# Both V gathers of a pair issued together in the gather phase of a hybrid decoder step

## The chip, the cores and the metric

The kernel runs on one core of one Trainium2 chip. The metric is the device time of one execution in microseconds. The program is one launch; its engines are PE (TensorE, matmuls), DVE (VectorE), ACT (ScalarE), POOL (GpSimd) and SP (SyncE, here only an issuer of DMAs). Each has its own instruction stream, and semaphores order them against each other.

## What is computed

One layer of a decoder trunk for 1024 prompt tokens and 8 sample tokens, model width 1024. A mixer (an SSD head group and an mLSTM head group) gives `x1`; then comes PEER, a layer that picks 128 experts (8 heads x 16) for each token out of 16384, and each expert is one row of `peer_u` and one row of `peer_v`:

```python
def _peer(x, wq, keys, u, v):            # cut to what matters
    ...
    eidx = jnp.take_along_axis(cidx, pos, axis=-1)      # 128 expert numbers per token
    gate = jax.nn.softmax(top, axis=-1)
    hid = gelu(einsum('td,thkd->thk', xb, jnp.take(u, eidx, axis=0)))
    return einsum('thk,thkd->td', gate * hid, jnp.take(v, eidx, axis=0))
...
x1 = _layer_norm(ALPHA * x + mix, ln1_g, ln1_b)
x2 = _layer_norm(ALPHA * x1 + _peer(x1, ...), ln2_g, ln2_b)
```

All is fp32. A row of `peer_u` or `peer_v` has 1024 numbers, 4 KB.

## The kernel before

Three parts run one after the other: the input projections and convolutions, the two scans with the output projection, and `build_peer`, which holds the change. Its first gather starts 967 us after the start of the span.

**Tiles of tokens.** The prompt is cut into 8 tiles of 128 tokens, the samples are a ninth. Five tiles (`GATHERED = 5`) are done by gathering: for one expert column of one tile, an indirect DMA fetches 128 rows, one for each token, into a buffer of 128 x 1024 (512 KB). The other three tiles are done densely: all of `peer_u` and `peer_v` pass in 128 blocks of 128 rows, with the gates of unpicked experts at zero.

**Slots.** The gather work is written as a loop over slots `t`, unrolled on each engine. Slot `t` handles the U column `t` (tile `t // 128`): POOL gathers the rows into `ub[t % 4]` (line 1597), and DVE multiplies them with the token's `x1` and sums (line 1833, the "dot" of the slot, semaphore `dot`). After 16 columns ACT takes the gelu and DVE multiplies the gate in (`wg`). 16 to 20 slots later the V column is gathered into `vbf[v % 4]` (`gather_v`, line 1572) and added with its weight.

**Two ways for V.** Up to slot 319 (`SD = 320`) V column `v = t - 20` is handled in slot `t`, so V columns 0 to 299 (`PE_ROWS = 300`), and PE does the sum: two columns make a pair, with half of the tokens of each in either buffer half, and in each odd slot PE multiplies the two rows of the pair with small diagonal matrices `dg` that ACT prepared and adds into PSUM (lines 2194 to 2206, semaphore `pv`, one count for each pair). That "V product" is 8 matmuls in the trace. From slot 320 on, DVE adds V rows itself (line 1873), and PE works on the dense blocks.

**Waits on POOL.** POOL issues its gathers in the order of the loop and each waits for its buffer. A U gather of slot `t` waits for the dot of slot `t - 4` (line 1593). A V gather `v` below 300 waits, through `v_free(v - 4)`, for the product of the pair to which `v - 4` belongs (line 1568):

```python
if 0 <= v < PE_ROWS:
    pool.wait_ge(s["pv"], v // 2 + 1)
```

As POOL's stream is in order, a gather that waits holds back all gathers behind it.

**Other work of these slots.** `background(t)` lays the mixing product, the normalisation, the scores and the top-16 picks of the coming tiles over the slots, in stretches of 36: PE does `mix` (line 2122) and `score` (line 2140), DVE the norm and the picks (lines 1620 to 1742). From slot 246 on, for slots up to 318, one-hot products build the gates of the dense tiles (`one_hots`, PE line 2248). SP loads what this needs, and from slot 300 on the first dense blocks.

Of the kernel before, what the change touches and what calls it, by code (L numbers as in the profile page):

```python
# [73 lines left out]
def free(eng, sem, value):  # L74

    if not isinstance(value, int) or value > 0:
        eng.wait_ge(sem, value)


def build(nc, a, o):  # L80
# [17 lines left out]
    with top:  # L98
# [451 lines left out]
        with ExitStack() as ctx:  # L550
            build_scan(nc, a, o, ctx, sem, PB, ident, two, wo, s_wo, s_pre, pre, mt0, cht_d, chs_d, tok_d, rows_d, rows_s_d, bc_d, mixt_d)
        end_phase()
        build_peer(nc, a, o, locals())


# [631 lines left out]
def build_peer(nc, a, o, L_):  # L1187
# [20 lines left out]
    LAG, LAG_PE, SD = TOPK, TOPK + 4, 320  # L1208
    PE_ROWS = SD - LAG_PE
# [17 lines left out]
    def v_rows(t):  # L1227

        if t < LAG_PE:
            return ()
        if t < SD:
            return (t - LAG_PE,)
        if t < SD + LAG_PE - LAG:
            v = PE_ROWS + 2 * (t - SD)
            return (v, v + 1)
        return (t - LAG,)

    def by_dve(v):  # L1240

        return max(0, v - PE_ROWS)
# [19 lines left out]
    with ExitStack() as ctx:  # L1262
# [106 lines left out]
        with nc.Block() as block:  # L1369
            @block.sync  # L1370
            def _(sp):
# [152 lines left out]
                for b in range(NBLK):  # L1524
                    if b + 4 < NBLK:
                        load_u(b + 4)
                    if b + 7 < NBLK:
                        load_v(b + 7)
                    if b % 8 == 1 and 8 < b < NBLK - 8:
                        load_g(b // 8 + 1)  # L1530
                    if block_slot(b) <= 386 < block_slot(b + 1):
                        sp.wait_ge(s["dot"], 3 * CH)
                        sp.wait_ge(s["acc0"], 1)
                        load_x1g(4)
                    if block_slot(b) <= 408 < block_slot(b + 1):
                        sp.wait_ge(s["ax"], by_dve(3 * CH))
                        load_gix(4)
                    if block_slot(b) <= 420 < block_slot(b + 1):
                        sp.wait_ge(s["pick"], NP - 1)
                        sp.wait_ge(s["mixg"], 4 * NP - 3)  # L1540
                        sp.wait_ge(s["x1st"], 16 * PICK[SAMPLE])
                        for n in range(3):
                            load_xs(n)
                    if block_slot(b) <= 560 < block_slot(b + 1):
                        sp.wait_ge(s["dot"], 4 * CH)
                        sp.wait_ge(s["acc0"], 3)
                        load_xs(3)
                        sp.wait_ge(s["stored"], 16 * 4)
                        load_xs(4)
# [7 lines left out]
            @block.gpsimd  # L1557
            def _(pool):
                nc.gpsimd.iota(iou, [[1, P]], 0, 0).then_inc(s["iou"], 1)
                pool.wait_ge(s["iou"], 1)  # L1560

                def gather(buf, table, index, done):
                    pool.indirect_dma_start(out=buf, out_offset=None, in_=a[table],  # L1563
                                            in_offset=bass.IndirectOffsetOnAxis(ap=index, axis=0)).then_inc(done, 16)

                def v_free(v):
                    if 0 <= v < PE_ROWS:
                        pool.wait_ge(s["pv"], v // 2 + 1)
                    elif v >= 0:
                        pool.wait_ge(s["ax"], by_dve(v + 1))  # L1570

                def gather_v(v):
                    n, h, k = v // CH % 2, v % CH // TOPK, v % TOPK
                    m, e = k // 2, k % 2
                    if v < CH and v % 32 == 0:
                        pool.wait_ge(s_gixv[0], 64 * (v // 32 + 1))
                    elif v % CH == 0 and v < PE_ROWS:
                        pool.wait_ge(s_gixv[n], 64 * (1 if n else 5))
                    v_free(v - NB)
                    pool.sem_inc(s["passed"], 1)  # L1580
                    at = 64 * e + 8 * h + m
                    gather(vbf[:, v % NB, :], "peer_v", (gixv if v < PE_ROWS else gixu)[n][:, at:at + 1], s_v[v % NB])

                for t in range(SLOTS):
                    c, h, k = t // CH, t % CH // TOPK, t % TOPK
                    if t < CH and t % 32 == 0:
                        pool.wait_ge(s["ix0"], t // 32 + 1)
                    if 0 < c < GATHERED and t % CH == 0:
                        pool.wait_ge(s_gix[c % 2], 16 * (c // 2 if c % 2 == 0 else (c + 1) // 2))
                    if t == U_SLOTS:  # L1590
                        pool.wait_ge(s["trc"], 1)
                    if t < U_SLOTS + NSMP:
                        free(pool, s["dot"], t - 3)
                    pool.sem_inc(s["passed"], 1)
                    if t < U_SLOTS:
                        at = 64 * (k % 2) + 8 * h + k // 2
                        gather(ub[:, t % NB, :], "peer_u", gixu[c % 2][:, at:at + 1], s_u[t % NB])
                    elif t < U_SLOTS + NSMP:
                        gather(ub[:, t % NB, :], "peer_u", ixs[:, t - U_SLOTS:t - U_SLOTS + 1], s_u[t % NB])
                    for v in v_rows(t):  # L1600
                        gather_v(v)
                    if t in (290, 292, 294, 296):
                        k = (t - 290) // 2
                        if k == 0:
                            pool.wait_ge(s["xdh"], 1)
                        nc.gpsimd.tensor_tensor(xds[:, 1, 2 * k:2 * k + 2, :], xraw[:, 2 * k:2 * k + 2, :],
                                                xds[:, 0, 2 * k:2 * k + 2, :].bitcast(f32), ALU.subtract).then_inc(s["xdlo"], 1)
                for b in range(NSMP):
                    if b < NB:
                        v_free(U_SLOTS - NB + b)  # L1610
                    else:
                        pool.wait_ge(s["dot"], U_SLOTS + NSMP)
                    pool.sem_inc(s["passed"], 1)
                    gather((vbf if b < NB else ub)[:, b % NB, :], "peer_v", ixs[:, b:b + 1], s_vs[b])

            @block.vector
            def _(dve):
# [126 lines left out]
                def norm2(r, step):  # L1744
                    y = acc[r]
                    if step == 1:
                        free(dve, s["ax"], by_dve((r + 1) * CH))
                        V.bn_stats(st7[:, 0, :], y[:, 0:512])
                        ch.link_plain(V.bn_stats(st7[:, 1, :], y[:, 512:D]))
                    elif step == 2:  # L1750
                        ch.link(V.bn_aggr(mv7[:, :], st7[:, :, :]))
                        V.tensor_scalar(mv7[:, 1:2], mv7[:, 1:2], EPS, None, ALU.add).then_inc(s["yvar"], 1)
                    elif step == 5:
                        dve.wait_ge(s["ysq"], r + 1)
                        ch.link(V.reciprocal(mv7[:, 1:2], mv7[:, 1:2]))
                    elif step == 7:
                        dve.wait_ge(s["gl1"], 32)
                        V.scalar_tensor_tensor(y, y, mv7[:, 0:1], gb1[:, :], ALU.subtract, ALU.mult).then_inc(s["ymul"], 1)
                        dve.wait_ge(s["ymul"], r + 1)
                    elif step == 12:  # L1760
                        dve.wait_ge(s["gl2"], 32)
                        V.scalar_tensor_tensor(y, y, mv7[:, 1:2], gb2[:, :], ALU.mult, ALU.add).then_inc(s["y"], 1)
# [594 lines left out]
```

## Time and profile before

| | us |
|---|---|
| median of 3 runs (3498.75 to 3521.03) | 3500.99 |
| span of the profiled execution | 3505.5 |
| first U gather | 967 |
| first and last V gather for PE | 1033.5 and 2113.2 |

| engine | busy us of the span | share |
|---|---|---|
| PE | 3153.1 | 90% |
| DVE | 2539.3 | 72% |
| POOL | 1752.3 | 50% |
| ACT | 951.9 | 27% |

The profile is of one execution. Times count from the start of its span. A gather on POOL (`DMA_INDIRECT`) is busy only while POOL makes its descriptors; the data moves afterwards, in the DMA engines, and its landing is seen where the engine that needs it starts. In a row of the view in order of time, the square bracket gives the idle time of the engine before the row and what ended it by the profile. "issue" means that nothing the profile shows was waited for.

### The profile page before, as it was taken

The numbers are of one execution on the slowest core, as the hardware profiler recorded it, in microseconds if no ns is written. First come the engines' busy times: TensorE is split into PE (matmuls) and PEld (weight loads), VectorE is DVE, ScalarE is ACT, GpSimd is POOL, SyncE is SP. The second block draws the span as 40 slices with busy tenths as digits, with TensorE's granted clock in tenths as the row PEclk, the third lists the DMA queues.
The fourth block names the chain that finished last, engine by engine and source line by source line (L and its number), as shares of the span: only waits on it lengthen the run. The fifth ranks groups of instructions, "written<-read, shape, count | busy, mean of one in ns | idle before, by whom it ended". The sixth has DMA issues, their size and how long they took to land.

```text
span 3505.5 us, 42684 instructions
## 1 busy us (share of the span) xinstructions
PE 3153.1 (90%) x13863; PEld 2084.0 (59%) x13863; DVE 2539.3 (72%) x5317; ACT 951.9 (27%) x2199; POOL 1752.3 (50%) x1420
## 2 busy tenths in 40 slices
PE   8989999999788888888868676999999999999998
PEld 8987887787332233233334345776676766767764
DVE  6662001799486888888899996777777777877777
ACT  3112222566111111111158882111111111111111
POOL 3341221344034666667665565555555555555553
PEclk9999999999899999999989888999999999999999
DMA  4324433788667999999998999999999999999996
GB/s 147 92 68 161 154 139 117 270 278 300 247 208 265 340 352 355 352 338 341 343 344 323 351 331 392 384 394 390 379 389 399 391 371 365 395 401 388 389 377 241
DMA packets 385327, 1074.38 MB, mean 306 GB/s; under 512 B 55128, under 2 KB 145144, under 8 KB 378848
## 3 DMA queue, kind: packets, MB, share of 16 engines
q0 software_dynamic: 186624, 679.56, 51.8%
q1 hardware_dynamic: 146592, 308.65, 24.4%
q10 hardware_dynamic: 51904, 83.63, 6.5%
q8 instruction: 102, 1.67, 0.2%
q14 instruction: 105, 0.86, 0.1%
HBM read 978.52 MB, written 93.05 MB: 306 GB/s over the span
## 4 chain that ended last, share of the span: by engine, by line
PE 41%; DMA 12%; DVE 8%; issue 7%; POOL 4%; ACT 2%; POOLq 0%; ACTq 0%; DVEq 0%
PE PB L2177 17%; PE PB L2164 14%; DMA vbf<-in_peer_v,gixv 6%; DMA x1d<-in_peer_u 4%; PE PB L2153 3%; PE PB L2204 3%; PE PB L2140 2%; DVE ub L1833 2%; POOL ub L1563 2%; DMA ub<-in_peer_u,gix 2%; POOL vbf L1563 2%; PE PB L2248 1%; ACT oha L1988 1%; PE PB L2122 1%; DVE ohb L1780 1%
## 5 line engine op out<-in xcount | busy, mean ns | idle before, releaser
L1563 POOL DMA_INDIRECT ub<-in_peer_u,gix x640 | 707.8, 1106 | 641.6 <-DVE hid L1833 432.8
L2177 PE MATMUL PB<-vbd,wd 128*128 128x512 f32 x1536 | 686.5, 597 | 0.0
L2164 PE MATMUL PB<-xds,uts 128*128 128x384 f32 x3072 | 569.4, 340 | 0.0
L2164 PEld LDWEIGHTS PB<-xds,uts 128*128 128x128 f32 x3072 | 531.7, 189 | 0.5 <-issue 0.5
L1563 POOL DMA_INDIRECT vbf<-in_peer_v,gixv x300 | 341.9, 1140 | 273.5 <-PE PB L2204 138.3
L1563 POOL DMA_INDIRECT vbf<-in_peer_v,gix x340 | 397.3, 1169 | 160.8 <-issue 98.7
L2177 PEld LDWEIGHTS PB<-vbd,wd 128*128 128x128 f32 x1536 | 284.6, 192 | 310.7 <-issue 310.7
L2204 PE MATMUL PB<-vbf,dg 128*64 128x512 f32 x1200 | 329.9, 673 | 136.6 <-DMA vbf<-in_peer_v,gixv 126.3
L1794 DVE TENSOR_TENSOR uts<-PB,uts 128x512 fp32r<-128x512 f32 x256 | 176.1, 688 | 304.7 <-ACT uts L2010 285.9
L1833 DVE CUSTOM_DVE_ANT_0 ub<-ub,x1g 128x1024 f32<-128x1024 f32 x257 | 313.7, 1223 | 79.0 <-DMA ub<-in_peer_u,gix 65.4
L2010 ACT CAST uts<-PB 128x512 fp32r<-128x512 f32 x256 | 150.3, 587 | 650.2 <-PE PB L2153 631.9
L1833 DVE CUSTOM_DVE_ANT_0 ub<-ub,x1gb 128x1024 f32<-128x1024 f32 x256 | 311.7, 1217 | 4.8 <-DMA ub<-in_peer_u,gix 4.6
L2204 PEld LDWEIGHTS PB<-vbf,dg 128*64 128x64 f32 x1200 | 88.4, 147 | 322.3 <-issue 312.3
L1873 DVE SCALAR_TENSOR_TENSOR acc<-vbf,wg,acc 128x1024 f32<-128x1024 f32 x212 | 271.3, 1280 | 4.8 <-DMA vbf<-in_peer_v,gix 3.7
L2140 PE MATMUL PB<-wp,x1T 128*128 128x512 f32 x576 | 270.7, 613 | 1.2 <-ACT x1T L1962 1.2
L2122 PE MATMUL PB<-wo,mt 128*128 128x512 f32 x528 | 248.9, 616 | 12.4 <-DVE x L1624 6.0
L2140 PEld LDWEIGHTS PB<-wp,x1T 128*128 128x128 f32 x576 | 106.7, 194 | 162.4 <-issue 162.4
L541 DVE TENSOR_REDUCE ssum<-smp 8x512 f32<-8x2048 f32 x6 | 23.0, 3828 | 242.6 <-ACT smp L419 242.6
L1833 DVE CUSTOM_DVE_ANT_0 ub<-ub,acc 128x1024 f32<-128x1024 f32 x128 | 156.4, 1227 | 54.3 <-DMA ub<-in_peer_u,gix 46.0
L2122 PEld LDWEIGHTS PB<-wo,mt 128*128 128x128 f32 x528 | 98.1, 195 | 163.9 <-issue 163.9
L2015 ACT ACTIVATE hg<-PB 128x384 f32<-128x384 f32 x128 | 62.9, 492 | 465.5 <-PE PB L2164 463.2
L2248 PE MATMUL PB<-oha,ohb 128*128 128x128 f32 x768 | 119.8, 308 | 74.0 <-DVE ohb L1780 50.9
(397 smaller groups left out, 5180.2 us busy)
## 6 DMA issues: line engine op xcount, KB each, us to landing
vbd<-in_peer_v SPq DMA_DIRECT2D x128, 512.0 KB
x1d<-in_peer_u SPq DMA_DIRECT2D x96, 512.0 KB
gd_d<-stag ACTq DMA_DIRECT2D x12, 2048.0 KB
gbd<-gd_d SPq DMA_DIRECT2D x16, 1536.0 KB
ubd<-in_peer_u SPq DMA_DIRECT2D x32, 512.0 KB
wtr<-in_w_tok SPq DMA_DIRECT2D x6, 2048.0 KB, 8.1
tok_d<-stg ACTq DMA_DIRECT2D x48, 256.0 KB, 2.0
rb_e<-rows_d SPq DMA_DIRECT2D x8, 1536.0 KB, 9.7
```

The source lines that it names most:

```text
L1563: pool.indirect_dma_start(out=buf, out_offset=None, in_=a[table], in_offset=bass.IndirectOffsetOnAxis(ap=index, axis=0)).then_inc(done, 16)
L1794: V.tensor_tensor(uts[:, b % 2, 1, 4 * x:4 * x + 4, :].rearrange("p k e -> p (k e)"), PB[:, 7, :], uts[:, b % 2, 0, 4 * x:4 * x + 4, :].re ...
L1833: V.tensor_tensor_reduce(out=ub[:, t % NB, :], in0=ub[:, t % NB, :], in1=by, scale=1.0, scalar=0.0, op0=ALU.mult, op1=ALU.add, accum_out=i ...
L1873: V.scalar_tensor_tensor(y, vbf[:, v % NB, :], wg[:, hv % 2, col:col + 1], y, ALU.mult, ALU.add).then_inc(s["ax"], 1)
L2010: S.copy(uts[:, b % 2, 0, 4 * x:4 * x + 4, :].rearrange("p k e -> p (k e)"), PB[:, 7, :]).then_inc(s["utc"], 1)
L2122: last = T.matmul(PB[:, 2 + h, :], mt[:, m % 2, j % 4, :], wo[:, j, h * 512:(h + 1) * 512], start=j == 0, stop=j == 15)
L2140: last = T.matmul(PB[:, 4 + n, :].rearrange("p (h n) -> p h n", h=4), x1T[:, kk, :], wp[:, 4 * n:4 * n + 4, kk, :], start=kk == 0, stop=kk ...
L2153: last = T.transpose(PB[:, 7, j * P:(j + 1) * P], ubd[b % 4][:, (4 * x + j) * P:(4 * x + j + 1) * P], ident[:, :])
L2164: last = T.matmul(PB[:, 6, 0:TD], uts[:, b % 2, ul, k, :], xds[:, xl, k, :], start=(k, n) == (0, 0), stop=(k, n) == (KD - 1, 2))
L2177: last = T.matmul(PB[:, 2 * d + n, :], wd[:, b % 2, d * CH:(d + 1) * CH], vbd[b % 8][:, n * 512:(n + 1) * 512], start=b == 0, stop=b == NB ...
L2204: last = T.matmul(PB[64 * g:64 * g + 64, x, :], dg[:, n % 2, g, :], vbf[:, (v0 + g) % NB, x * 512:(x + 1) * 512], start=v0 % CH == 0, stop ...
L2248: last = T.matmul(PB[:, 2 + m % 2, :].rearrange("p (b t) -> p b t", t=4)[:, :, x], ohb[:, m % 2, x, :], oha[:, m % 2, x, :], start=True, s ...
```

## The change

A new function `v_issues` gives the V columns that POOL issues in slot `t`, in place of `v_rows` in POOL's loop alone. For V columns below 300 it gives both columns of a pair in the pair's even slot, and none in the odd slot; for all later slots it gives what `v_rows` gives.

```diff
+    def v_issues(t):
+
+        v = t - LAG_PE
+        if 0 <= v < PE_ROWS:
+            return (v, v + 1) if v % 2 == 0 else ()
+        return v_rows(t)
...
-                    for v in v_rows(t):
+                    for v in v_issues(t):
                         gather_v(v)
```

`LAG_PE` is 20, so `v` is even where `t` is. The slots in which ACT, DVE and PE handle V columns are still those of `v_rows`.

POOL's stream at the first V columns (slot 20), before; `ub` rows are U gathers, `vbf` rows V gathers:

```order
L1563 DMA ub<-in_peer_u,gix 128x1024 x21
L1563 DMA vbf<-in_peer_v,gixv 128x1024
L1563 DMA ub<-in_peer_u,gix 128x1024
L1563 DMA vbf<-in_peer_v,gixv 128x1024
L1563 DMA ub<-in_peer_u,gix 128x1024
L1563 DMA vbf<-in_peer_v,gixv 128x1024
```

The same place after the change:

```order
L1570 DMA ub<-in_peer_u,gix 128x1024 x21
L1570 DMA vbf<-in_peer_v,gixv 128x1024 x2
L1570 DMA ub<-in_peer_u,gix 128x1024 x2
L1570 DMA vbf<-in_peer_v,gixv 128x1024 x2
L1570 DMA ub<-in_peer_u,gix 128x1024 x2
```

The second V gather of a pair has moved ahead of one U gather, that of the odd slot; two U gathers now follow each other, and two V gathers.

POOL's stream at slots 318 to 321 (the last V columns for PE), before, with the numbers of the rows:

```order
703 L1563 DMA ub<-in_peer_u,gix 128x1024
704 L1563 DMA vbf<-in_peer_v,gixv 128x1024
705 L1563 DMA ub<-in_peer_u,gix 128x1024
706 L1563 DMA vbf<-in_peer_v,gix 128x1024 x2
707 L1563 DMA ub<-in_peer_u,gix 128x1024
708 L1563 DMA vbf<-in_peer_v,gix 128x1024 x2
```

And after the change:

```order
404 L1570 DMA vbf<-in_peer_v,gixv 128x1024 x2
405 L1570 DMA ub<-in_peer_u,gix 128x1024 x2
406 L1570 DMA vbf<-in_peer_v,gix 128x1024 x2
407 L1570 DMA ub<-in_peer_u,gix 128x1024
408 L1570 DMA vbf<-in_peer_v,gix 128x1024 x2
```

From the rows with `in_peer_v,gix` on, both streams are the same. On PE, DVE, ACT and SP no row has moved.

## Rows read from the trace of the kernel before

**Rows 1.** Busy time by window: length, PE, PEld, DVE, ACT, POOL, clock, DMA share, GB/s.
```profile
1030.00:1085.00 55.00, 48.95 (x126) 21.20 (x128) 33.92 (x120) 9.39 (x21) 20.18 (x21) 0.93 0.58 200
1085.00:1250.00 165.00, 136.16 (x386) 48.12 (x383) 135.02 (x437) 29.71 (x77) 108.31 (x98) 0.94 0.94 343
1250.00:1800.00 550.00, 458.91 (x1316) 163.43 (x1315) 464.23 (x1547) 103.00 (x268) 374.86 (x340) 0.96 0.95 347
1800.00:2114.00 314.00, 226.39 (x1100) 135.51 (x1099) 286.24 (x824) 258.83 (x668) 181.02 (x147) 0.86 0.91 337
2140.00:3400.00 1260.00, 1239.37 (x5308) 881.50 (x5309) 969.36 (x1345) 204.02 (x389) 718.25 (x633) 0.99 1.01 387
```

**Rows 2.** Waits of POOL, 1085 to 1800: in total, times, longest. All rows.
```profile
POOL vbf L1563 <- issue: 68.8, 173, 1.9
POOL ub L1563 <- issue: 65.1, 210, 1.4
POOL vbf L1563 <- PE PB L2204: 59.5, 27, 5.6
POOL vbf L1563 <- DVE hid L1833: 34.5, 18, 4.4
POOL ub L1563 <- PE PB L2204: 2.7, 9, 0.3
```

**Rows 3.** Longest waits of PE and of DVE, 1085 to 1800.
```profile
PE PB L2204 <- DMA vbf<-in_peer_v,gixv: 116.7, 80, 5.6
...
DVE ub L1833 <- DMA ub<-in_peer_u,gix: 85.9, 73, 4.0
```

**Rows 4.** Groups by line, 1085 to 1800: busy, mean ns, idle time before them.
```profile
L1563 POOL DMA_INDIRECT ub<-in_peer_u,gix x219 | 242.1, 1106 | 67.8 <-issue 65.1 <-PE PB L2204 2.7
L1563 POOL DMA_INDIRECT vbf<-in_peer_v,gixv x218 | 241.1, 1106 | 162.8 <-issue 68.8 <-PE PB L2204 59.5 <-DVE hid L1833 34.5
```

**Rows 5.** POOL in order of time: start, length, operation, idle before it.
```profile
1243.15 1.39 POOL L1563 DMA_INDIRECT vbf<-in_peer_v,gixv  x1 [2.28 <-PE PB L2204]
1244.85 1.58 POOL L1563 DMA_INDIRECT ub<-in_peer_u,gix  x1 [0.30 <-issue]
1246.73 0.94 POOL L1563 DMA_INDIRECT vbf<-in_peer_v,gixv  x1 [0.30 <-issue]
...
1257.21 0.94 POOL L1563 DMA_INDIRECT vbf<-in_peer_v,gixv  x1 [1.50 <-DVE hid L1833]
1258.45 0.94 POOL L1563 DMA_INDIRECT ub<-in_peer_u,gix  x1 [0.30 <-issue]
```

**Rows 6.** PE in order of time, same place.
```profile
1248.98 4.02 PE L2140 MATMUL PB<-wp,x1T 128*128 128x512 f32 x8
1254.47 1.94 PE L2204 MATMUL PB<-vbf,dg 128*64 128x512 f32 x8 [1.46 <-DMA vbf<-in_peer_v,gixv]
```

**Rows 7.** DVE in order of time, same place.
```profile
1252.43 1.23 DVE L1833 CUSTOM_DVE_ANT_0 ub<-ub,x1g 128x1024 f32<-128x1024 f32 x1 [1.89 <-DMA ub<-in_peer_u,gix]
```

**Rows 8.** POOL and DVE in order of time, first U gather and first dot.
```profile
966.73 1.15 POOL L1563 DMA_INDIRECT ub<-in_peer_u,gix  x1 [48.77 <-DVE gix L1732]
...
971.15 1.23 DVE L1833 CUSTOM_DVE_ANT_0 ub<-ub,x1g 128x1024 f32<-128x1024 f32 x1 [4.88 <-DMA ub<-in_peer_u,gix]
```

**Rows 9.** POOL and DVE in order of time, first stage.
```profile
1059.42 0.94 POOL L1563 DMA_INDIRECT vbf<-in_peer_v,gixv  x1 [13.49 <-PE PB L2204]
...
1066.08 1.23 DVE L1833 CUSTOM_DVE_ANT_0 ub<-ub,x1g 128x1024 f32<-128x1024 f32 x1 [12.41 <-DMA ub<-in_peer_u,gix]
...
1082.58 1.22 DVE L1833 CUSTOM_DVE_ANT_0 ub<-ub,x1g 128x1024 f32<-128x1024 f32 x1 [6.20 <-DMA ub<-in_peer_u,gix]
```

**Rows 10.** Waits of PE and DVE, 1800 to 2114.
```profile
PE PB L2248 <- DVE ohb L1780: 50.9, 22, 5.6
...
PE PB L2204 <- DMA vbf<-in_peer_v,gixv: 9.6, 4, 2.7
...
DVE ub L1833 <- DMA ub<-in_peer_u,gix: 2.5, 2, 2.1
```

## The prediction, as written before the changed kernel ran

> **What bounds the kernel now.** I read the busy time by stage first [rows 1]. The change touches only the slots in which a U gather and a V gather for TensorE alternate on POOL, from about 1033 to 2114 us. That part has three stages. From 1033 to 1085 PE is nearly always busy (48.95 of 55 us) while the DMA engines are at 0.58. From 1085 to 1800, 715 us, no engine is full: PE 595 us (0.83), DVE 599 us (0.84), but the DMA engines are at 0.94 and 0.95 and move 343 and 347 GB/s. From 1800 to 2114 the one-hot work is added, and DVE is busy 286 of 314 us. Afterwards the dense blocks run with PE at 0.98 and DMA at 1.01 and 387 GB/s.
>
> Then I asked the middle stage who waits for whom. PE waited 116.7 us in 80 places for a V row to land and DVE 85.9 us in 73 places for a U row [rows 3]; PE waited for little else. POOL, which issues both, waited for the V product of PE (59.5 us) and, by the label, for DVE (34.5 us) [rows 2]. The label is not to be taken at its word: the gather at 1257.21 is put down to DVE, yet it starts 0.80 us after the V product ends (1254.47 + 1.94 = 1256.41), just as other V gathers do behind a product [rows 5, 6]. A V gather waits for no dot product in the code, so these waits too are for PE.
>
> That gives a loop. The even V gather of pair n+2 waits for the product of pair n, which waits for the odd V row of pair n. One turn, written out [rows 5, 6]: even gather at 1243.15, a U gather, odd gather at 1246.73, its end at 1247.67, product 6.80 us later at 1254.47, 1.94 us of product, 0.80 us, next gather at 1257.21. That is 14.06 us for four slots. The stage's mean is 715 us for 218 slots [rows 4], 3.28 us a slot or 13.1 us for four, so the turn shown is an ordinary one.
>
> **How much POOL waits.** In the stage it issued 219 + 218 gathers, 483 us busy, with 230.6 us of idle time ahead of them [rows 4]. Back to back, 0.30 us lies between two gathers [rows 5], 131 us in all. The other 99.5 us are waits for V buffers, 14% of the stage.
>
> **The change part by part.** No instruction is added or taken away; 300 U and 300 V gathers remain, and PE, DVE, ACT and SP keep their order. In each pair of slots the odd V gather passes ahead of one U gather.
>
> The free wait of the odd V gather costs nothing where it now stands: it asks for the same pair as the even gather's, which has just passed. What is issued between two even gathers stays four gathers.
>
> *The gain.* The odd V row is issued earlier by one gather: 1.106 us (242.1/219) and 0.30 us of gap, 1.41 us [rows 4]; in the turn shown it would be 1.58 + 0.30 = 1.88 us [rows 5]. The loop gets shorter by that, if landing takes as long as before. With 218/4 = 54.5 turns, 54.5 x 1.41 = 77 us is the upper bound, inside the 99.5 us that POOL waits.
>
> *What takes part of it back.* The 6.80 us from issue to product are not a constant: with nothing else in flight the first U row of the phase was used 3.27 us after its gather ended (967.88 to 971.15) [rows 8]. The other 3.5 us are mainly a queue in front of the DMA engines (and sometimes PE's own work), and it grows when POOL issues faster. The DMA engines were busy 0.94 x 165 + 0.95 x 550 = 678 of 715 us [rows 1]; if a gather costs them the same time as now, 37 us can be won and no more. By bytes the bound is looser: 346 GB/s now against 387 in the dense stage gives 715 x (1 - 346/387) = 76 us. The two ends are thus 37 and 76-77 us. I go by the share, because it is of this very stage and this mix, and because the dense stage also has the blocks of SP's queue in flight. Of the 37 us I take three quarters, 28 us (my choice): the buffers are finite and slots with long DVE work will still let the DMA engines run dry.
>
> *The U row that is passed.* The U gather of the odd slot comes 1.24 to 1.41 us later, its dot product too, and with 599/218 = 2.75 us of DVE work a slot the even slot's dot also moves. Who waits for a dot is the U gather four slots on, and behind it all of POOL. In the same turn: U gather at 1244.85, dot from 1252.43 to 1253.66, next U gather of that buffer at 1258.45 [rows 5, 7]. Of these 4.79 us the release takes about 0.8, as behind a product; 4.0 us are slack. The delay takes 1.41 and a loop shortened by 28/54.5 = 0.5 us takes that; 2 us are left. Cost 0; bound below.
>
> *First stage.* The V gather at 1059.42 waited 13.49 us for a product that PE, busy with other work, came to late [rows 1, 9]. A row that is there earlier helps nothing. The U gather behind it moves 1.24 us, and so does the dot at 1066.08; the next wait of DVE (6.20 us, at 1082.58) covers it. 0, at most +1.2 us.
>
> *One-hot stage.* PE waited 9.6 us for V rows but 50.9 for DVE's one-hots, and DVE waited 2.5 us for U rows [rows 10]. DVE sets the pace. 0; bounds: 9.6 us gained, a few lost.
>
> *Behind 2140 us.* Order unchanged, PE and DMA full; the stage only starts earlier. 0.
>
> **Sum.** 3505.5 us of span - 28 = 3477.5. The median of the runs is 3501.0, 4.5 us under that execution's span, so I forecast 3473 us.
>
> **Rivals.**
>
> *A, nothing comes of it (chance 0.22, -8 to +12 us, about 3501).* The DMA engines are in truth full: 0.95 is as high as gathers alone get, and each row that is asked for earlier stands longer in the queue. For it: windows of the stage at 0.94 and 0.95 throughout. Against it: 387 GB/s later [rows 1], and POOL's waits, during which nothing is issued. The page "DMA: Bandwidth & Descriptors" of the Trainium skill, section "Bandwidth", has HBM bind a core at about 358 GB/s; by that figure 346 would be 97% of all there is and the gain at most 24 us. The dense stage's 387 over 1260 us does not agree with it, so the sum does not use it.
>
> *B, the whole loop is won (0.14, 50 to 77 us, about 3435).* The queue does not grow, the byte bound holds, PE's waits go, and its V products keep their fast form (1.94 us) more often. It is decided by whether the share stays below 1 while the rate rises to some 370 GB/s and more.
>
> *C, slower (0.12, +8 to +50 us, about 3525).* The U loop takes over from the V loop. U rows now arrive in twos: the odd one 1.41 us late, and DVE, already waiting 85.9 us for U rows, waits longer for it; if its next work is long, the even dot slips too, and POOL then stands at a U gather with two V gathers behind. In full that is 54.5 x 1.41 = 77 us lost; less the 28 us gained, +49. It decides where the 4.0 us of slack fall below about 2 us. For it: DVE waits for U rows nearly as much as PE for V rows. Against it: among all of POOL's waits of the stage [rows 2] no U gather waits for DVE, so that slack is not used up anywhere so far.
>
> **How the numbers follow.** The forecast, a gain of 12 to 50 us, has 0.52; its own range is 3451 to 3489. About 1% (35 us) is what a measurement of this kernel can tell. Of the forecast's 0.52 I put a third above 35 us of gain: 0.17, and with B's 0.14 the chance of faster is 0.31. Of C half is above +35 us: 0.06 slower. The rest, 0.63, is the same within 1%. The range 3436 to 3510 leaves out B's top (0.05) and most of C (0.11).
>
> **What would show it.** On POOL, even to odd V gather should be about 1.24 to 1.5 us apart (3.58 in the turn shown), and the idle time ahead of V gathers in the middle stage should fall from 162.8 us to about 130. PE's waits for V rows should fall from 116.7 us to about 90, DVE's for U rows stay near 86 or rise a little. The middle stage should take about 687 us, at a DMA share of 0.98 and some 360 GB/s; the one-hot stage should stay at 314 and the dense stage at its length. I am wrong if the share is up but the rate is not (A), if POOL shows waits of U gathers for dots of tens of us (C), or if the middle stage loses over 50 us (B). If the one-hot stage changes by over 10 us, the reading of DVE as its pace is wrong.

## The result, and the profile after

| | before | changed |
|---|---|---|
| median of 6 runs | 3502.28 us | 3477.69 us |
| span of the profiled execution | 3505.5 us | 3477.7 us |
| from slot 30 to slot 249 (219 slots, "middle stage") | 716.7 us | 689.0 us |
| from slot 249 to slot 318 (one-hot stage) | 304.2 us | 303.1 us |
| from slot 319 to the end | 1393.6 us | 1391.6 us |

The ratio is 0.9925, 95% interval 0.9895 to 0.9954. One of the six runs of the changed kernel took 6372.1 us; it counts in the median (3475.8 us without it) and neither in the ratio nor in its interval. 24.6 us are gone by the medians, 27.8 by the spans. The stages are measured between the starts of U gathers in the view in order of time; slots 0 to 30 took 117.1 us after 118.2 before, and the first gather starts 1.9 us later. So in this pair of profiles 27.7 us came from the middle stage and what the other stages gave and took cancels out. A second profile of the changed kernel (e11, below) divides the gain a little differently.

Busy time of the changed kernel by window, for [rows 1] (length, PE, PEld, DVE, ACT, POOL, granted clock, DMA share, GB/s):

```profile
1030.00:1086.00 56.00, 50.21 (x130) 21.58 (x132) 34.41 (x120) 9.16 (x20) 21.78 (x21) 0.93 0.58 199
1086.00:1771.00 685.00, 592.52 (x1694) 207.62 (x1690) 595.34 (x1970) 131.66 (x345) 473.02 (x437) 0.95 0.97 361
1771.00:2088.00 317.00, 229.66 (x1113) 137.81 (x1112) 291.59 (x845) 259.00 (x671) 175.03 (x149) 0.86 0.92 338
2114.00:3374.00 1260.00, 1239.45 (x5312) 881.42 (x5313) 969.39 (x1345) 203.99 (x389) 712.74 (x634) 0.99 1.00 387
```

The work of PE and DVE in the middle stage is nearly the same (592.5 and 595.3 us busy, 595 and 599 before), done in less time, and the DMA engines went from 0.95 and 347 GB/s to 0.97 and 361.

Groups by line on POOL, 1086 to 1771, for [rows 4] (busy, mean ns, idle time before them):

```profile
L1570 POOL DMA_INDIRECT ub<-in_peer_u,gix x219 | 239.1, 1092 | 96.5 <-issue 70.5 <-DVE hid L1840 19.5 <-PE PB L2211 6.5
L1570 POOL DMA_INDIRECT vbf<-in_peer_v,gixv x218 | 234.3, 1075 | 115.8 <-issue 71.7 <-PE PB L2211 30.0 <-remote 14.0
```

Waits of POOL in the same stretch (in total, times, longest; all rows), for [rows 2]:

```profile
POOL vbf L1570 <- issue: 71.7, 194, 7.0
POOL ub L1570 <- issue: 70.5, 195, 2.4
POOL vbf L1570 <- PE PB L2211: 30.0, 16, 3.7
POOL ub L1570 <- DVE hid L1840: 19.5, 12, 2.4
POOL vbf L1570 <- remote: 14.0, 8, 2.5
POOL ub L1570 <- PE PB L2211: 6.5, 12, 1.4
```

Waits of PE and of DVE, for [rows 3]:

```profile
PE PB L2211 <- DMA vbf<-in_peer_v,gixv: 61.3, 35, 5.9
PE PB L2129 <- DVE x L1631: 18.0, 4, 4.6
PE PB L2211 <- issue: 5.1, 7, 1.3
PE PB L2129 <- issue: 4.2, 1, 4.2
...
DVE ub L1840 <- DMA ub<-in_peer_u,gix: 65.9, 51, 6.6
```

PE's wait for V rows is halved (116.7 to 61.3 us), DVE's for U rows has fallen too (85.9 to 65.9), and two waits are new: U gathers that wait for a dot (19.5 us in 12 places), and PE's mixing product (L2129), which waits 22.2 us in 5 places, 18.0 us of it by the label for DVE's normalisation (3.5 us in all before).

One turn of the loop in the changed kernel, POOL and then PE in order of time:

```profile
1223.62 0.93 POOL L1570 DMA_INDIRECT vbf<-in_peer_v,gixv  x1 [0.97 <-PE PB L2211]
1224.86 0.93 POOL L1570 DMA_INDIRECT vbf<-in_peer_v,gixv  x1 [0.30 <-issue]
1226.10 1.50 POOL L1570 DMA_INDIRECT ub<-in_peer_u,gix  x1 [0.31 <-issue]
...
1235.16 0.94 POOL L1570 DMA_INDIRECT vbf<-in_peer_v,gixv  x1 [0.30 <-issue]
```
```profile
1231.87 1.94 PE L2211 MATMUL PB<-vbf,dg 128*64 128x512 f32 x8
```

The odd gather starts 1.24 us behind the even one, where the turn in [rows 5] had 3.58. Its end at 1225.79, the product 6.08 us later at 1231.87, 1.94 us of product, and the next gather of that buffer at 1235.16: 11.54 us for four slots against the 14.06 of the prediction's example. Both are single turns. The mean over pairs 6 to 113, worked out from the start times of gathers and products, tells more (us):

| | even to odd gather | odd gather busy | its end to the product | product | product's end to the next even gather | turn |
|---|---|---|---|---|---|---|
| before | 2.82 | 1.16 | 5.74 | 2.15 | 1.21 | 13.07 |
| changed | 1.44 | 1.01 | 6.22 | 2.09 | 1.78 | 12.54 |

The first two columns give 1.53 us a turn, the third takes 0.48 back, the last before the total 0.57. What stays is 0.53 us a turn, and 54.5 turns of that are 29 us.

The third column is not landing time alone. Before, PE stood waiting for the row in 79 of these 108 turns, with 5.71 us in the mean from the gather's end to the product. In the changed kernel it stood waiting in only 36, with 6.03 us; in the other 72 the product came behind other work of PE, 6.32 us after the gather's end (29 turns and 5.82 us before).

### The profile page after: what moved, and what is told of

Read it like the earlier page. It is cut to its first block, busy times and chain, and to the rows that moved or that the text cites. A ratio compares the mean times of both kernels' runs of the same rounds, so it can differ in the third digit from the quotient of the medians.

```text
span 3477.7 us, 42684 instructions
## 1 busy us (share of the span) xinstructions
PE 3150.0 (91%) x13863; PEld 2080.3 (60%) x13863; DVE 2540.7 (73%) x5317; ACT 949.0 (27%) x2199; POOL 1730.9 (50%) x1420
## 3 DMA queue, kind: packets, MB, share of 16 engines
q1 hardware_dynamic: 146592, 308.65, 24.6%
## 4 chain that ended last, share of the span: by engine, by line
PE 39%; DVE 11%; DMA 10%; issue 7%; POOL 4%; ACT 2%; another core or an unknown queue 0%; ACTq 0%; POOLq 0%; DVEq 0%
PE PB L2184 16%; PE PB L2171 13%; DMA x1d<-in_peer_u 5%; DVE ub L1840 3%; PE PB L2160 3%; PE PB L2211 3%; DMA ub<-in_peer_u,gix 2%; PE PB L2147 2%; POOL vbf L1570 2%; POOL ub L1570 2%; DMA vbf<-in_peer_v,gixv 2%; PE PB L2129 2%; DVE ohb L1787 1%; DVE oha L1785 1%; PE PB L2255 1%
## 5 line engine op out<-in xcount | busy, mean ns | idle before, releaser
L1570 POOL DMA_INDIRECT ub<-in_peer_u,gix x640 | 699.4, 1093 | 678.1 <-DVE hid L1840 462.5
L1570 POOL DMA_INDIRECT vbf<-in_peer_v,gixv x300 | 331.9, 1106 | 222.2 <-PE PB L2211 114.7
L2129 PE MATMUL PB<-wo,mt 128*128 128x512 f32 x528 | 256.5, 632 | 31.4 <-DVE x L1631 22.1
L2129 PEld LDWEIGHTS PB<-wo,mt 128*128 128x128 f32 x528 | 100.1, 199 | 184.1 <-issue 184.1
```

The source lines that it names most:

```text
L2129: last = T.matmul(PB[:, 2 + h, :], mt[:, m % 2, j % 4, :], wo[:, j, h * 512:(h + 1) * 512], start=j == 0, stop=j == 15)
```

## The experiments

Three sets of four kernels ran, each set beside its own runs of the kernel before (medians 3492.6, 3499.8 and 3505.8 us); a ratio is always to those. The middle stage of each is again that from slot 30 to slot 249 of its profile. Line numbers shift by a few between kernels.

### Where: the one-hot stage alone

```diff
-        if 0 <= v < PE_ROWS:
+        if 226 <= v < PE_ROWS:
             return (v, v + 1) if v % 2 == 0 else ()
```

> V rows paired only from slot 246 on (V columns 226 to 299), alternating before that. Theory (DVE sets the pace of the one-hot stage): nothing, 3495-3508 us; middle stage 717 us, the 314-317 us of the one-hot stage unchanged within 4 us. Rival (the V loop limits that stage too, POOL waits 53 us for PE there): 5 to 15 us faster.

Measured: 3481.87 us, ratio 0.9977 (0.9948 to 1.0005). In its profile the middle stage, unchanged code, takes 716.9 us, and the one-hot stage, changed code, 304.4 against 304.2. Both windows:

```profile
1077.00:1792.00 715.00, 601.91 (x1713) 212.37 (x1709) 604.01 (x1997) 135.71 (x354) 474.43 (x438) 0.95 0.95 347
1792.00:2105.00 313.00, 223.22 (x1087) 134.91 (x1086) 281.76 (x806) 254.63 (x660) 170.69 (x145) 0.86 0.91 333
```

By the profile the one-hot stage gives nothing. The ratio is not as sharp: its centre is 8 us faster and its interval ends just above 1, so the rival of that expectation (5 to 15 us faster) isn't excluded. The later profiles lean that way too. From slot 249 to slot 318 the six with pairs in the even slot throughout take 298.3 to 303.1 us, the four that alternate with four V buffers 304.2 to 315.5. So the stage gives little, perhaps some 5 us. In the changed kernel PE there waits for DVE's one-hots as it did in [rows 10], only longer, while the wait for V rows is down from 9.6 us to 1.0:

```profile
PE PB L2255 <- DVE ohb L1787: 69.3, 30, 6.3
...
PE PB L2211 <- DMA vbf<-in_peer_v,gixv: 1.0, 1, 1.0
```

### Where in the slots: the pair in its odd slot

```diff
-            return (v, v + 1) if v % 2 == 0 else ()
+            return (v - 1, v) if v % 2 else ()
```

> Both V rows of a pair together, but in the pair's odd slot: the even V row is one U gather later than before, the odd one stays behind its U gather. Between two waits for a V product POOL's order is as in the changed kernel (V, V, U, U). Theory (V loop): the loop is as short, middle stage 685-695 us, time 3470-3485 us. Rival (what counts is that the rows are there earlier against PE's and DVE's slots): nothing is there earlier and the even row is later, so 3500-3520 us.

Measured: 3464.52 us, ratio 0.9921 (0.9892 to 0.9950). Here it is the even row that is issued later; the odd one keeps its place. The gain is that of the change all the same; it was expected at 3470 to 3485 us and came out lower. So what counts is not how early the odd row is issued against its slot, but how much is issued between the two rows of a pair. The middle stage of its profile was short, 675.9 us, with no wait of PE for the normalisation; the same order with the mixing product moved (e16, below) took 689.4 with an equal ratio, so I lay no weight on the 675.9.

### Which loop: a fifth buffer for V or for U rows

A fifth row buffer takes 4 KB in each partition of the on-chip memory. I made the room by leaving out the biases of both layer norms, with the gain standing in for them, so these kernels do not compute the layer. That alone is the control; then either kind was given a fifth buffer, first in the order of the kernel before.

The control:

```diff
-        gb1, gb2 = sb("gb1", [P, D]), sb("gb2", [P, D])
+        gb1 = sb("gb1", [P, D])
+        gb2 = gb1
...
-                wide(gb2[:, :], "ln1_b", s["gl2"])
```

> The kernel before with nothing but the bias of both layer norms left out (two loads of 512 KB fewer, gb1 used in place of gb2): the control for the runs with a fifth buffer. Expected of all theories: middle stage 714-719 us, time within 5 us of before. If it is 10 us or more faster, that much of those runs is not the buffer's.

Measured: 3495.72 us, ratio 0.9988 (0.9962 to 1.0013); middle stage 704.0 us in its one profile. The control costs or gives next to nothing by the ratio. That its profile is 13 us shorter in the stage is a warning: between profiles of kernels with the same medians the stage can differ by that much.

The control, and a fifth V buffer:

```diff
-                    v_free(v - NB)
+                    v_free(v - NV)          # NV = 5
...
-                    gather(vbf[:, v % NB, :], "peer_v", ..., s_v[v % NB])
+                    gather(vb[v % NV], "peer_v", ..., s_v[v % NV])
```

> The order of before, but with a fifth V buffer (its room comes from leaving out the bias of both layer norms: gb2 is neither loaded nor kept, gb1 stands in for it, so y is not the reference's). Even V gathers now wait for the product three pairs back, odd ones for that two pairs back, so the loop from V gather to V product no longer holds POOL up. Theory (V loop): the middle stage, 219 slots, falls from 717 us to 670-690 although U and V gathers still alternate, POOL's idle time ahead of V gathers falls from 163 us to under 130, and the time is 3455-3480 us. Rival (adjacency: two gathers of one table in a row are cheaper for POOL or the DMA engines): no change, 3495-3505 us.

Measured: 3442.02 us, ratio 0.9856 (0.9818 to 0.9893), the best of all kernels here: 1.3% below the control, ratio against ratio (they ran in different sets). Middle stage 672.4 us:

```profile
1081.00:1752.00 671.00, 582.38 (x1689) 205.25 (x1688) 596.11 (x1971) 131.49 (x342) 472.68 (x438) 0.96 0.98 368
```

Its U and V gathers alternate as before the change, so the gain needs no two gathers of one table next to each other, which was the rival here (3495 to 3505 us). With five buffers the even row need not wait for the product that the odd one waits for, so no issue time lies in the loop; its mean turn is 12.28 us.

The control, and a fifth U buffer:

```diff
-                    free(pool, s["dot"], t - 3)
+                    free(pool, s["dot"], t - NU + 1)          # NU = 5
...
-                    gather(ub[:, t % NB, :], "peer_u", ..., s_u[t % NB])
+                    gather(ur[t % NU], "peer_u", ..., s_u[t % NU])
```

> The order of before with a fifth U buffer, bias left out. V loop theory: the V loop still holds POOL up, so a U buffer more is worth little: middle stage 708-718 us against 717. Rival (any buffer more lets more gathers be in flight, whichever it is): as with the fifth V buffer, 670-685 us.

Measured: 3501.30 us, ratio 0.9999 (0.9975 to 1.0023), middle stage 719.6 us. On POOL the V gathers wait as long as before, 165.7 us against the 162.8 in [rows 4]:

```profile
L1565 POOL DMA_INDIRECT vbf<-in_peer_v,gixv x218 | 245.1, 1124 | 165.7 <-PE PB L2206 76.8 <-issue 67.0 <-DVE hid L1835 21.9
```

So it is not "one row more in flight" that helps. One V row more gives 1.3%, one U row more gives nothing: the kernel before was held by the V loop, as the prediction read it from the trace.

### Together with the change

The order of the change with either fifth buffer. First the control, the fifth V buffer and the order of the change:

> As the run with the fifth V buffer, and with the pairs issued together (bias left out in the same way). Theory (V loop, with the DMA engines behind it): the two do not add. The changed order alone has a middle stage of 689 us at a DMA share of 0.97; here 675-690 us, the time 3462-3480 us, within 10 us of the run with the fifth buffer and alternating order. Rival (two separate gains, adjacency and buffers): 25 us below the fifth-buffer run in alternating order.

Measured: 3467.71 us, ratio 0.9922 (0.9894 to 0.9950), middle stage 693.9 us. The control, the fifth U buffer and the order of the change:

> The changed order (V, V, U, U) with a fifth U buffer in place of a fifth V buffer; the bias of both layer norms is left out in the same way, to have the room. Open since the fifth V buffer: alternating order gave a middle stage of 672 us, pairs with the same buffers 694. Theory (late U row: passing a U gather costs some 20 us in the middle stage, because the U loop, gather to dot to gather, becomes the one that holds): a U buffer more takes that cost away, middle stage 665-680 us against 689, POOL's waits of U gathers for DVE (19.5 us) gone. Rival (the DMA engines are the ceiling for pairs): 685-692 us. Rival (PE now runs ahead of DVE and waits for its normalisation, 18 us): 685-692 us, and that wait stays.

Measured: 3481.93 us, ratio 0.9957 (0.9933 to 0.9981), middle stage 691.0 us. And the changed kernel once more in that set, with no edit:

> The changed kernel once more, on the same chip as the other three. Middle stage 685-693 us if the first profile was typical; the ratio to before 0.990-0.995.

Measured: 3469.56 us, ratio 0.9917 (0.9881 to 0.9954), middle stage 695.1 us. Against the profile before, this second profile of the changed kernel has 21.6 us less in the middle stage and 5.9 us less in the one-hot stage (298.3 us). The windows of the two fifth buffers and of the repeat, in this order:

```profile
1084.00:1776.00 692.00, 589.24 (x1690) 206.25 (x1688) 597.14 (x1975) 131.56 (x347) 476.16 (x439) 0.95 0.96 358
```
```profile
1079.00:1768.00 689.00, 588.60 (x1699) 207.45 (x1699) 596.48 (x1971) 132.87 (x351) 468.90 (x439) 0.95 0.97 360
```
```profile
1073.00:1766.00 693.00, 597.62 (x1696) 208.97 (x1693) 598.10 (x1985) 132.15 (x349) 471.54 (x438) 0.93 0.96 358
```

In the order of the change neither buffer adds anything. With the fifth V buffer the time was expected within 10 us of the alternating kernel; it is 25.7 us above it, and no run of the one reaches a run of the other (3432.4 to 3452.7 us alternating, 3456.5 to 3475.7 in pairs, in one set). With the fifth U buffer the median is 12 us above that of the changed kernel in its set. The fifth U buffer did take away the new waits of U gathers, and the V gathers took them over. Its V gathers and its U gathers (in four buffers, and in the fifth, `ube`) on POOL:

```profile
L1572 POOL DMA_INDIRECT vbf<-in_peer_v,gixv x220 | 239.3, 1088 | 153.6 <-issue 74.9 <-PE PB L2213 48.9 <-remote 28.0
L1572 POOL DMA_INDIRECT ub<-in_peer_u,gix x176 | 187.4, 1065 | 53.7 <-issue 52.2 <-PE PB L2213 1.5
L1572 POOL DMA_INDIRECT ube<-in_peer_u,gix x43 | 43.9, 1022 | 13.1 <-issue 12.8 <-PE PB L2213 0.3
```

Idle time of POOL beyond the 0.30 us of each gather was 30.2 us before U and 50.6 before V gathers in the changed kernel, 80.8 us in all, and 29.0 and 60.1 in its repeat, 89.1 in all; with the fifth U buffer it is 0.5 and 86.9, 87.4 in all. The sum has not fallen.

### PE's new wait for the normalisation

With the fifth buffers ruled out, the largest new item was PE's wait for DVE. One of the 5 places in the changed kernel:

```profile
1303.75 1.94 PE L2211 MATMUL PB<-vbf,dg 128*64 128x512 f32 x8 [1.40 <-ACT dg L2047]
1310.27 3.75 PE L2129 MATMUL PB<-wo,mt 128*128 128x512 f32 x4 [4.58 <-DVE x L1631]
1313.95 2.38 PE L2211 MATMUL PB<-vbf,dg 128*64 128x512 f32 x8
1317.15 1.87 POOL L1570 DMA_INDIRECT vbf<-in_peer_v,gixv  x1 [3.72 <-PE PB L2211]
```

PE has got ahead of DVE, stands 4.58 us, needs 3.75 us for the next product, and POOL waits 3.72 us behind it. The total of such waits, those labelled "issue" at the same line included, was 22.2 us in the changed kernel, 20.7 in its repeat, 21.5 and 22.5 with the fifth V and U buffer, and at most 6.6 in the kernels that alternate or put the pair in its odd slot. That looked like the cap. PE's mixing product was put two slots later in each stretch:

```diff
-                            if 2 <= at <= 12:
-                                mix(q + 2, at - 2)
+                            if 4 <= at <= 14:
+                                mix(q + 2, at - 4)
```

On the changed kernel:

> The changed kernel with one edit on PE: in each stretch of 36 slots the first eleven steps of the mixing product stand in slots 4 to 14 of the stretch, not 2 to 12, so that PE does not come to them before DVE has emptied their PSUM bank. Open: every kernel with pairs in the even slot stays at a middle stage of 689-695 us, whichever fifth buffer it has, while alternating order with a fifth V buffer reached 672; in all of the first kind, and in none of the others, PE waits 21-22 us in 5 places, 4.5 us each, for the normalisation of DVE. Theory (PE ahead of DVE): with the mixing later these waits go, its V products are not held up, and the middle stage falls to 668-680 us, the time to about 0.986-0.988 of before. Rival (the waits are slack that PE would spend elsewhere, the DMA engines or DVE bound pairs): waits go, but V waits grow by as much, 686-695 us.

Measured: 3471.38 us, ratio 0.9915 (0.9889 to 0.9940), middle stage 697.4 us. On the kernel before:

> The kernel before with the same edit on PE, its gathers alternating. In it PE waits only some 2-4 us for that normalisation. Theory (PE ahead of DVE is a matter of pairs in the even slot): no gain, 712-720 us in the middle stage, ratio 0.998-1.003. Rival (the mixing is better placed there in any order): as large a gain as in the changed order, 15 us or more.

Measured: 3508.20 us, ratio 1.0002 (0.9979 to 1.0025), middle stage 713.3 us. With the fifth V buffer and pairs:

> Pairs in the even slot, a fifth V buffer (bias of both layer norms left out) and the mixing two slots later. Without the last it had a middle stage of 694 us, alternating order with the fifth buffer 672. Theory (PE ahead of DVE): the whole difference is that wait, so 668-678 us. Rival (pairs cost the U loop something too, POOL waited 34 us for dots): it stays above 682 us.

Measured: 3466.71 us, ratio 0.9893 (0.9858 to 0.9928), middle stage 697.5 us. With the pair in its odd slot:

> Both V rows in the odd slot, and the mixing two slots later. In the odd slot PE is not ahead of DVE and hardly waits for its normalisation (1.5 us). Theory: no further gain over the odd slot alone (676 us, ratio 0.992), 672-682 us, and no better than pairs in the even slot with the mixing later. Rival (the edit on PE gives a gain of its own): 660-670 us.

Measured: 3473.44 us, ratio 0.9921 (0.9888 to 0.9954), middle stage 689.4 us.

The theory fell. In the first of these the wait for the normalisation is gone from PE's list, and PE waits 93.4 us for V rows in its place, 32 us more than the changed kernel:

```profile
PE PB L2211 <- DMA vbf<-in_peer_v,gixv: 93.4, 55, 5.6
PE PB L2211 <- issue: 5.7, 6, 2.5
```

PE idle for DVE and PE idle for a row were the same idle time under two names. The same edit under the fifth V buffer was to bring the stage to 668 to 678 us; it stayed at 697.5, above the 682 us of that expectation's rival.

**What stays open.** In the order of pairs the stage takes 689 to 698 us in seven of the eight profiles, whichever buffer is added and wherever the mixing product stands (675.9 in the eighth, the odd-slot one); alternating with a fifth V buffer it takes 672, in its one profile. The ratios of the two kernels with the fifth V buffer in one set, 0.9856 and 0.9922, have intervals that just don't meet; that of pairs with the mixing product later, 0.9893, overlaps the better one. So the difference is likely real and its size is uncertain. I can't name what makes the difference. It isn't the rate of the DMA engines, since 368 GB/s were reached.

The rows do show where the time lies on POOL. U gathers of the alternating kernel with the fifth V buffer, and of the pairs with it:

```profile
L1565 POOL DMA_INDIRECT ub<-in_peer_u,gix x219 | 245.7, 1122 | 97.9 <-issue 64.1 <-DVE hid L1835 20.4 <-PE PB L2206 11.0
L1572 POOL DMA_INDIRECT ub<-in_peer_u,gix x219 | 239.7, 1094 | 113.7 <-issue 69.9 <-DVE hid L1842 34.3 <-PE PB L2213 9.5
```

Beyond the 0.30 us of each gather POOL waits 34.2 us before V gathers in the first and 35.6 in the second, but 31.4 and 47.2 before U gathers; with the fifth V buffer, pairs and the mixing product later it is 35.3 and 49.6. So what the pairs lose against the alternating order stands almost wholly before U gathers, and more of it waits for dots. With the fifth U buffer in place of the V buffer all the waiting stands before V gathers (86.9 us). This fits the rival of e15's expectation, that pairs make the U loop tighter too: with a fifth buffer in one loop the other holds. It isn't shown, as no run had a fifth buffer in both.

An idea that fits the same rows is that rows now come in twos: two U rows land together and then two V rows, so that DVE and PE each have a longer stretch with nothing landing, and four buffers of each kind bridge less of it. That is argued only. A fifth buffer of both kinds at once would tell; it wasn't tried. No kernel that computes the whole layer came out ahead of the changed one by more than the intervals allow.

## Why the prediction was right, and where it wasn't

The time forecast was 3473 us and the median is 3477.7; the span was to be 3477.5 and is 3477.7. The total is closer than the working behind it deserves: the ceiling in it was wrong, and the three quarters that I took of it happened to make up for that.

**The bound and the loop: right, and shown.** The kernel before was held by the V loop: a fifth V buffer gave 1.3%, a fifth U buffer nothing. The part of the "DVE" label that belongs to PE was read rightly too: of the 18 V gathers that [rows 2] put down to DVE, 14 start 0.80 to 0.87 us after the end of the very product that they wait for in the code, and the other four 1.5 to 4.5 us after it.

**The shortening of 1.41 us a turn: right.** In the table of means the odd gather starts 1.38 us sooner behind the even one and is 0.15 us shorter itself, 1.53 in all.

**What the issue-to-product time takes back: right in kind, half of it mis-placed.** I had all of the difference between 77 and 28 us go into a longer queue. The time from the odd gather's end to the product grew by 0.48 us a turn, 26 us over 54.5 turns, and only part of that is landing: where PE stood waiting for the row it grew by 0.32 us (5.71 to 6.03), and in 72 turns instead of 29 the row had to wait for PE. Another 0.57 us a turn, 31 us, went into time between the product and the next even gather, which now more often stands behind other gathers on POOL's stream: before, POOL went on within 1.0 us of the product in 60 of 108 turns, now in 31.

**The ceiling of 37 us by the DMA share: wrong.** The step that failed is its condition, that a gather costs the DMA engines the same busy time as now. Share times window was 679 us before for 437 gathers, 1.55 us each; it is 664 us in the changed kernel, 1.52 each, and 658 us with the fifth V buffer, 1.50 each. Two kernels won more than 37 us in the stage: the fifth V buffer 44 us (716.7 to 672.4), and the pair in its odd slot 41 us (675.9). The windows of the latter and of the control:

```profile
1080.00:1755.00 675.00, 580.03 (x1692) 205.62 (x1690) 596.85 (x1973) 132.15 (x344) 459.99 (x437) 0.97 0.98 366
1072.00:1775.00 703.00, 586.80 (x1701) 208.57 (x1697) 599.51 (x1984) 134.72 (x351) 477.84 (x438) 0.97 0.96 352
```

Each is one profile, and against the control's own profile (704.0) the fifth V buffer won only 32 us; by the ratios it is 1.3% of the whole, 46 us. The rate is the firmer sign: from a share of 0.95 to 0.98 it rose by 6% (347 to 368 GB/s), more than the rounding of the shares can hide. Of my two ends, 37 and 76 us, only the byte bound held. Three quarters of 37 gave the right 28 by luck: had I taken three quarters of 76, I would have forecast 57. Rival A fell with it. The Trainium skill's page "DMA: Bandwidth & Descriptors", section "Bandwidth", which rival A cites, has about 358 GB/s as the side of HBM that binds a core, and says in the same section that this is each core's part when both cores of an HBM domain stream. This program runs on one core, and its profiles go above the figure: 361 and 368 GB/s over some 680 us each, and 387 over 1260 us.

**The late U row at cost 0: wrong.** I had 2 us of slack left for the U gather four slots on, and nothing waiting. In the changed kernel U gathers wait 30.2 us beyond their 0.30 each, in 26 places over half a microsecond, where before it was 1.3 us in one place. One of them, the view of POOL in order of time:

```profile
1241.01 1.62 POOL L1570 DMA_INDIRECT ub<-in_peer_u,gix  x1 [2.42 <-DVE hid L1840]
```

It is rival C's mechanism, of which I wrote that 4.0 us of slack, read in one turn, spoke against it. One turn was too few to read a slack from. But the passed U row is not all of the cause: alternating with the fifth V buffer, where nothing is passed, U gathers wait 31.4 us too, in 21 places, and that kernel is the fastest. POOL running ahead is enough to bring such waits. Nor are they a price that can be subtracted: with the fifth U buffer they vanish and the time stays. They lie in parallel with waits for V buffers.

**PE's waits: mis-sized.** Forecast about 90 us for V rows, measured 61.3, and 22.2 for DVE that I hadn't thought of; 92.5 us of idle time ahead of PE's V and mixing products in all, against 125.5 before. Which name PE's idle time bears depends on the order, and its sum follows the stage's length only roughly: the odd-slot profile, 13 us shorter in the stage, has 94.4 us.

**POOL and DVE.** Idle before V gathers: forecast 130, measured 115.8 us. DVE's wait for U rows: forecast 86 or a little more, measured 65.9. The second moved the other way than I wrote ("near 86 or rise a little"). All idle time ahead of gathers fell from 230.6 to 212.3 us, part of the V gathers' share having moved to U gathers. POOL's busy time fell as well, from 483.2 to 473.0 us for the same 437 gathers, which I hadn't thought of; what makes a gather shorter there isn't known.

**First and dense stage at 0: right; one-hot stage at 0: nearly.** 117.1 after 118.2, 303.1 after 304.2, and 1391.6 after 1393.6 us. The repeat's 298.3 us and the ratio of the run with the one-hot stage alone leave room for a few us of gain in the one-hot stage, inside the bound of 9.6 us. In the first stage the wait of a V gather for the busy PE stands as in [rows 9]:

```profile
1060.41 0.93 POOL L1570 DMA_INDIRECT vbf<-in_peer_v,gixv  x1 [12.88 <-PE PB L2211]
```

**Rival B, the whole loop:** no profile of the middle stage reached its 50 us. Even 368 GB/s, with no issue time left in the loop, gave 44 us.

## What to carry to other kernels

Where a buffer is freed by an operation that needs two transfers, look for the closed loop of issue, landing, use and release, and take out what is issued between the two; here that alone was worth 0.8%, and whether the pair stood early or late in its slots made no difference that the ratios show. Of a shortened loop expect only a part (here 0.53 of 1.53 us a turn) when other loops and the DMA queue are nearly as tight, and bound it by the bytes, not by the DMA busy share. Before blaming a new wait for what is missing, take it away: twice here the wait vanished and its time turned up under another name.

## What was unexpected of the hardware

- **The DMA share understates what is left near its top.** In one stage with one mix of gathers: 347 GB/s at 0.95, 361 at 0.97, 368 at 0.98. The engines' busy time for 437 or 438 gathers fell from 679 to 658 us.
- **PE after a stop.** After 4.58 us of idle time four matmuls took 3.75 us, in a stretch with the granted clock at 0.50 (1.2 GHz); the same four took 1.98 us at a granted clock of 1.00 (2.4 GHz), 10 us earlier. The two windows hold length, PE, PEld, DVE, ACT, POOL, clock, DMA share and GB/s:

```profile
1300.37 1.98 PE L2129 MATMUL PB<-wo,mt 128*128 128x512 f32 x4
```
```profile
1300.30:1302.40 2.10, 2.05 (x6) 0.68 (x4) 2.00 (x10) 0.91 (x3) 1.15 (x1) 1.00 1.01 398
1310.20:1314.10 3.90, 3.83 (x6) 1.32 (x8) 3.75 (x19) 1.87 (x3) 2.63 (x3) 0.50 1.03 411
```

  So a wait of 4.58 us cost PE some 6.4.
- **POOL stalls that belong to no release.** In the middle stage of the changed kernel 14 gathers started late though their product or dot had long ended, 17.7 us in all, part of it under the label "remote", which the kernel before doesn't have. Before it was 11 places and 11.7 us, with the fifth V buffer alternating 20 and 28.7, with the fifth U buffer in pairs 20 and 33.8. The number of buffers alone doesn't set it: with the fifth U buffer alternating it is 6 places and 10.0 us, with no "remote". It is the kernels in which products hold POOL up less that have more of it. What POOL waits for there isn't known.
